# A decode-and-prompt attention layer on one core: unit outputs in four 32-column strips, decode transposes at the end of their step, five unread products taken out

## The reference

```python
o_a = gg[..., 0:1] * o_c + gg[..., 1:2] * o_s + gg[..., 2:3] * o_w     # compressed, selected, sliding window
s = (einsum('bqhc,bsc->bhqs', q_lat, c) + einsum('bqhr,bsr->bhqs', q_pe, kr)) * MLA_SCALE
o_lat = einsum('bhqs,bsc->bqhc', softmax(mask(s)), c)                   # latent attention
pa = (o_a * silu(ga)) @ w_proj_a;  pb = (o_b * silu(gb)) @ w_proj_b
h = sigmoid(ma) * pa + sigmoid(mb) * pb
y = x + rmsnorm(h @ w_out, norm_post)
```

## Time and profile before

| | |
|---|---|
| runs | 743.08, 744.10, 747.31 us, median 744.1 |
| span of the profiled execution | 739.6 us (its time outside the span is not recorded; the three runs are 3.5 to 7.7 us longer) |
| TensorE busy | 692.4 us of 739.6 |
| VectorE, ScalarE, GpSimd busy | 440.6, 211.5, 123.4 us |
| DMA | 170.27 MB, mean 230 GB/s |
| bound for "faster" or "slower" here | 0.5% of 744.1, 3.7 us |

### The profile page before, as it was taken

How to read it: one execution, slowest core, us unless ns; L and a number is a source line. 1 busy time by engine, 2 the same in 40 slices (tenths; PEclk the granted TensorE clock), 3 DMA queues, 4 the chain that set the end, 5 groups by cost and what they waited for, 6 DMA issues and landing times.

```text
span 739.6 us, 14391 instructions
## 1 busy us (share of the span) xinstructions
PE 692.4 (94%) x5305; PEld 443.7 (60%) x5305; DVE 440.6 (60%) x1233; ACT 211.5 (29%) x579; POOL 123.4 (17%) x130
## 2 busy tenths in 40 slices
PE   9997999999988979789999999899999999999996
PEld 4443444644555655467675676557778888885452
DVE  3297799478666756764654554542577565644244
ACT  0302215555334434433533442321110101110111
POOL 0343340113042230321412202320000000000000
PEclk9999999999999999999999999999999999999998
DMA  9999994951779999967755686996210303026011
GB/s 343 414 414 421 418 399 159 384 219 49 250 276 336 315 381 343 393 222 277 276 209 185 237 285 232 332 334 259 72 57 1 114 1 114 1 91 280 29 47 41
DMA packets 57367, 170.27 MB, mean 230 GB/s; under 512 B 7537, under 2 KB 7690, under 8 KB 50514
## 3 DMA queue, kind: packets, MB, share of 16 engines
q1 hardware_dynamic: 47352, 120.68, 45.1%
q0 software_dynamic: 9600, 48.38, 16.6%
q10 hardware_dynamic: 346, 0.29, 0.1%
HBM read 164.99 MB, written 8.52 MB: 235 GB/s over the span
## 4 chain that ended last, share of the span: by engine, by line
PE 75%; DMA 9%; DVE 5%; issue 5%; SPq 3%; ACT 2%; another core or an unknown queue 1%; DVEq 0%; ACTq 0%
PE bank L1423 18%; PE bank L855 7%; PE bank L1463 7%; PE bank L1266 7%; DMA W<-w_attn 4%; PE bank L1153 4%; PE bank L1132 3%; PE bank L1250 3%; PE bank L1235 3%; PE bank L1018 3%; PE bank L1140 3%; DMA projP<-x 2%; PE bank L1200 2%; PE bank L1455 2%; DMA ring<-latent 2%
## 5 line engine op out<-in xcount | busy, mean ns | idle before, releaser
L710 POOL DMA_INDIRECT KRR<-krT,idxi x64 | 61.2, 957 | 221.9 <-PE bank L1239 207.1
L855 PE MATMUL bank<-W,XG 128*128 128x494 f32 x192 | 85.2, 589 | 4.2 <-DMA W<-w_attn 3.7
L1484 ACT ACTIVATE projP<-bank 128x128 f32<-128x128 f32 (+5 forms) x87 | 33.9, 391 | 110.0 <-PE bank L1423 47.5
L2438 DVE TENSOR_TENSOR projP<-projP,bank 128x260 f32<-128x260 f32 x83 | 33.9, 422 | 45.1 <-PE bank L1423 44.4
L855 PEld LDWEIGHTS bank<-W,XG 128*128 128x128 f32 x192 | 35.8, 195 | 41.0 <-issue 39.8
L1266 PE MATMUL bank<-W 128*128 128x260 f32 x256 | 60.4, 389 | 0.0
L1484 ACT ACTIVATE W<-bank 128x512 f32<-128x512 f32 (+2 forms) x69 | 40.1, 582 | 69.8 <-PE bank L898 18.7
L1670 ACT ACTIVATE projP<-bank,projP 128x128 f32<-128x128 f32 (+3 forms) x96 | 49.7, 524 | 29.9 <-DVE projP L2140 29.5
L2140 DVE CUSTOM_DVE_ANT_0 bank<-bank,maskb 128x128 f32<-128x128 f32 (+3 forms) x96 | 45.8, 507 | 15.9 <-PE bank L1132 11.2
L1266 PEld LDWEIGHTS bank<-W 128*128 128x128 f32 x256 | 47.3, 190 | 10.4 <-issue 3.3
L1463 PE MATMUL bank<-ring,W 128*128 128x512 f32 x112 | 49.5, 594 | 1.3 <-issue 1.3
(11 more groups left out here) (439 smaller groups left out, 1145.7 us busy)
## 6 DMA issues: line engine op xcount, KB each, us to landing
ring<-latent SPq DMA_DIRECT2D x200, 256.0 KB
XG<-latent SPq DMA_DIRECT2D x56, 256.0 KB
W<-w_gate SPq DMA_DIRECT2D x12, 1024.0 KB, 4.7
W<-w_attn SPq DMA_DIRECT2D x16, 494.0 KB, 9.8
ring<-w_out SPq DMA_DIRECT2D x2, 2048.0 KB
o_win<-win SPq DMA_DIRECT2D x1, 4088.0 KB
W<-xT SPq DMA_DIRECT2D x1, 2080.0 KB, 11.2
projP<-x SPq DMA_DIRECT2D x1, 2048.0 KB
```

Of the source, the lines that this page charges most:

```text
L710: pool.indirect_dma_start(out=dst, out_offset=None, in_=src, in_offset=bass.IndirectOffsetOnAxis(ap=idxi[:, col:col + 1], axis=0)).then_in ...
L855: mm = pe.matmul(bank[2 * (u % 2) + n][:, 0:GW], XG[:, k * TOK + tl * P:k * TOK + (tl + 1) * P], w_part(half, k, n), start=(k == 0), stop= ...
L1484: return act.activation(dst, src, ACT.Copy, scale=scale)
```

## The change

Four edits:

1. `outputs`: each unit's output product is cut into two of 32 stationary columns, so that the pair has four strips of 32 partitions where it had two of 64. The moving operand (128 columns) and the sums are the same; 240 products become 480.
2. `dec_transposes(d)` stands at the end of step `d`, behind the transposes and the last keys, and no longer in step `d + 1` behind the scores; except in the steps of `TURN_LATE` (those before step 15 and those with a gate), where it stays. Twelve chunks move: those of steps 16, 17, 20, 22, 24, 28, 32, 36, 40, 42, 44 and 46. In 16, 24, 28, 32 and 36 it then stands right behind the last key block.
3. The five products of L1230 are gone.
4. On VectorE `read_out` stands ahead of `dec_fold` in a step.

```diff
+        TURN_LATE = {d for d in SOFT_at if d + 1 < 16 or d in G_at}
...
                 for kb in range(tl + 1):
-                    for e in range(2):
-                        mm = pe.matmul(bank[3][64 * e:64 * e + 64, 0:P], values(br, tl, kb, h + e), PTb[e][:, kb * P:(kb + 1) * P],
+                    for strip in range(4):
+                        e, lo = strip // 2, 32 * (strip % 2)
+                        mm = pe.matmul(bank[3][32 * strip:32 * strip + 32, 0:P], values(br, tl, kb, h + e)[:, lo:lo + 32], PTb[e][:, kb * P:(kb + 1) * P],
                                        start=(first and kb == 0), stop=(last and kb == tl))
...
-                if i2 == 0 and p2 in KEPT_BUSY:
-                    pe.matmul(bank[5][:, :], ident, qrT[:, 0:512], start=True, stop=True)
                 job_landed(pe, J_MLA + m)
...
-            KEPT_BUSY = (6, 12, 13, 14, 15)
...
                 if d < PAIRS:
                     scores(d)
-                if d - 1 in SOFT_at:
+                if d - 1 in TURN_LATE:
                     dec_transposes(d - 1)
...
                 if d in K_at:
                     dec_keys(d, 3)
+                if d in SOFT_at and d not in TURN_LATE:
+                    dec_transposes(d)
...
+                if 2 <= d < PAIRS + 2:
+                    read_out(d - 2)
                 if d in OUT_at:
                     dec_fold(OUT_at[d])
                 if d == 0:
                     new_tokens()
-                if 2 <= d < PAIRS + 2:
-                    read_out(d - 2)
```

## The result

The changed kernel took 762.66 us (median of four runs, 759.33 to 764.26), the kernel before beside it 744.68 (743.08 to 747.31): a ratio of 1.0227 with a 95% interval of 1.0188 to 1.0266. It is 18 us slower, where 2.9 us faster was forecast, and outside the range.

The account below looks back on a forecast made before the run. TensorE's time was taken to bound the kernel. The terms 6.4 - 1.2 - 3.7 + 1.4 gave 2.9 us faster, so a median of 744.1 - 2.9 = 741.2 us, with a range from 733 to 748.5.

Parts of the forecast that it names:

- the 1.36 us of the earlier trace: End of step 36: TensorE's idle time before the decode transpose, read as waiting for ScalarE's copy of the last key group.
- Edit 1, array time and tiling: Unit outputs: same array time, 0.11 us saved per tiling change at 58 of 66 handovers, 6.4 us faster; bounds 0 and 7.3.
- rival D: Unit outputs: four strips don't run side by side where key blocks accumulate into one bank; 13.4 us more, 754.6; chance 0.02.
- Edit 1, the number of instructions: Unit outputs: 480 more records, as many weight loads, cost 2.3 us or nothing; half taken, 1.2 us slower.
- Edit 2: Twelve moved decode transposes: scores queue behind them in steps with keys and step 22; net 3.7 us slower.
- the place in step 36: Transpose starts 2.8 us after the last key block as before; scores follow it, 1.7 to 2.5 us later than before.
- Rival A: Decode transposes: moving them costs nothing, so the waits' 4.0 us go; 737.2, down to 730.8; chance 0.30.
- B's 12 us: Rival B, decode transposes: all twelve moved groups delay the scores, 1.0 us each, 12 instead of 3.7; 749.5; chance 0.11.
- Edit 3: Five unread products, 4.8 us in all: removing them brings 1.4 us, as loads take the rest; bounds 0 and 4.8.
- Rival C: TensorE's clock falls more often without unread products and with unsplit idle time; three more falls cost 5.1 us, 746.3; chance 0.15.
- The sign that I had named: TensorE's clock: more than one new stretch at 1.2 GHz would show the prediction wrong.
- Theory S: From the experiments: the unit outputs' doubled instructions reach TensorE late, it stands still, and the clock falls behind it.

Follow-up runs that it names:

- filler: Kernel before with three waits on long-reached semaphores ahead of each unit output product, 271 more TensorE instructions: 753.2 us against 744.4, ratio 1.0103.
- group B: Runs timed together: edit 1 alone, and the changed kernel with one edit taken back in each of three; the kernel before took 723.0 us.
- group C: Runs timed together: changed kernel again, empty waits added, edits 2 and 4 alone, unread products out alone; the kernel before took 744.4 us.
- after_b: The changed kernel as it is, in a group where the kernel before took 720.9 us: 718.2 us, ratio 0.9965.
- turn_late: Changed kernel with all decode transposes one step later, as before the change: 716.2 us against 723.0 for the kernel before, ratio 0.9901.
- strips_only: Kernel before with edit 1 alone, four 32-column strips: 714.9 us against 723.0, ratio 0.9879.
- kept_out: Kernel before without the five unread products: 746.4 us against 744.4, ratio 1.0038.
- moved_only: Kernel before with edits 2 and 4, strips and unread products as before: 749.7 us against 744.4, ratio 1.0068.
- after_again: The changed kernel repeated word for word: 765.5 us against 744.4 for the kernel before, ratio 1.0268.

## Why the prediction was wrong, point by point

**What bounds the kernel** was read rightly: TensorE's time. But I read "issue" rows as a property of the code. The profile of before had 14.9 us of TensorE's idle time without a named releaser, in 20 pieces; the rows and the 1.36 us of the earlier trace rows are of this kind. All six profiles from the 744 us condition have 12 to 17 us of it, the fourteen from the 722 us condition 0 to 3.8. These rows, and the 18 us of "remote" on VectorE and ScalarE, were the sign that this execution ran in a condition in which TensorE's counts come late and part of them isn't recorded.

**Edit 1, array time and tiling: right in the 722 us condition.** 0.89 us from scores to outputs as forecast. Forecast -6.4 without the price for instructions, bounds 0 and -7.3; measured -5.4 to -8.1 in four groups of the 722 us condition. My rival D (strips not side by side) is out.

**Edit 1, the number of instructions: this is the step that failed.** I priced it at 1.2 us from 3.2 us of idle time in 666 records, with 2.3 as the upper bound. In the 722 us condition the price is near 0, within some 3 us. In the 744 us condition the filler's 271 empty instructions cost 8.8 us alone (by the interval of the ratio 3 to 12), more than the 2.3 that I had as the most for 960, and what the changed kernel loses beyond the other edits, with the strips' gain of 7.3 counted, is 18.0 to 21.1 - 5.3 - 2.0 + 7.3, again 18 to 21 us, for 960 instructions; a rest, not a measurement. The fault is in the way the bound was made: I took the mean idle time per record of one line as linear and complete, where the cost comes as late counts of TensorE's semaphores, up to 5.4 us each, for which ScalarE, VectorE and then TensorE itself wait, with falls of the clock behind them. The earlier trace rows alone held 6.3, 11.2 and 6.5 us in which TensorE wasn't busy. The quotient also mixed two stretches, 3.2 us from 440 to 510 and 666 records from 448 to 510; with the 821 records of the same stretch it is 1.9 us.

**Edit 2: right.** Forecast +3.7; measured, with edit 4 in it, +3.0 (group B) and +5.3 (group C), and the place in step 36 behaves as said. The 2.8 us from the last keys to the transpose there were themselves stretched by a late count: in after_b it is 1.48 us (405.92 to 407.40). Rival A, that it costs nothing, is out, and so is B's 12 us.

**Edit 3: wrong in sign, small in size.** Forecast -1.4; measured +1.3 in group B (with edit 4 in it, and not beyond its uncertainty) and +2.0 in group C (the products alone, 0.01% to 0.74%). The loads take part of the 4.8 us back as forecast: in the changed kernel the first latent scores of the last jobs wait for their load.

```profile
517.31 1.08 PE L1235 MATMUL bank<-ring,projP 128*32 128x128 f32 x32 [3.47 <-DMA ring<-latent]
...
523.32 0.92 PE L1235 MATMUL bank<-ring,projP 128*32 128x128 f32 x25 [1.53 <-DMA ring<-latent]
```

What I missed is that the clock takes more: turn_late, which differs from strips_only by the missing products and edit 4, has 13.7 us at 1.2 GHz where strips_only has 6.8, and kept_out has 23.9 where the profile of before has 10.2. At half speed 6.8 us more is a loss of 3.4. The profiled execution of turn_late is the slowest of its six, but the mean granted clock of all runs says the same: 0.985 against 0.989 for strips_only, and 0.977 (ten runs) for kept_out against 0.984 for the kernel before beside it. Over 740 us the latter is 5.0 us, and the rest of kept_out's time is 2.1 shorter.

**Rival C, the clock falls,** named the right mechanism with a chance of 0.15 and a wrong size. I allowed three more stretches and 5.1 us; there were six more with 30.8 us, 13.7 us of TensorE's work by the balance above. The sign that I had named, more than one new stretch, came true. The trigger that I gave (missing products, an idle piece no longer split by the scores) is a part of it. In group C the missing share of the clock times the span, a mean over all runs, is 12.3 us before, 14.4 in moved_only, 17.3 in kept_out, 19.2 in the filler and 30.3 in the changed kernel. So of its 21 us 18 go with the clock, and each of the three single changes moves it, though these parts needn't add up.

**The condition.** Nothing in the times of before (743.08 to 747.31) showed that the kernel also runs in 722 us; I had no run of the other level. In the 722 us condition the sum comes out (-2.9 forecast, -2.7 measured; its parts, -7.3 for the strips on the mean of four groups, +3.0 and +1.3, make -3.0), but that is luck in part: edit 3 came out 2.7 us worse than forecast, and what makes up for it is that the strips came out 0.9 better, edit 2 0.7 better, and that the 1.2 us for instructions weren't due there.

**What is shown and what is argued.** Shown: the level of 744 or 722 us changes the sign of the change; in the one, empty instructions cost 8.8 us, in the other nothing within some 3 us; the time is lost in stops of TensorE, VectorE and ScalarE that end with a late count of TensorE's, and in the clock behind them; the late counts grow with TensorE's added instructions and not with the other edits.

Argued: that the strips have the whole rest of the 18 to 21 us, since they never met this condition alone.

Theory S as it was put, that instructions reach TensorE late, is not borne out: at the three long stops the products whose counts are missing are on record as started before the stop. Nor do the instruction transfers bear it out. Of the stops of over 0.8 us, 7 of 10 begin between 0.5 us before and 2.5 us behind the start of one of the 16 KB transfers in the changed kernel (7 of 12 in after_again), where the 32 transfers of the stage cover under a third of its time in this way. But in the profile of before it is 2 of 8, in the filler 2 of 11, in moved_only 4 of 8 and in kept_out 4 of 9, and those transfers took about 1.1 us in either condition. The Trainium skill's page "Runtime: NRT & Kernel Launch", section "Instruction fetch mechanics", says that the engine fetches its instructions itself in blocks of 16 KB and that crossing a block is mostly hidden. The 722 us condition agrees (0 to 3.8 us of unnamed idle time); for the 744 us condition no run here shows what holds the counts back.

What makes the condition stays open as well. One rival stands untested: the recording itself. Each time here is of an execution whose clock was recorded, and in the 744 us condition the record has lost about a fifth of the semaphore counts. No run shows whether the counts come late in an execution that isn't recorded.

## What to carry to other kernels

Look at TensorE's idle time with no named releaser, and at "remote" on the engines that read its banks, before pricing anything: where they are more than a few us, the profile may be from a condition in which an added instruction costs far more than its array time, and the kernel should be timed in other groups before a change is judged. Price extra instructions by an empty filler of the same number, not by a mean over records. And when an idle time is named after VectorE or ScalarE, see whether that engine had itself been standing still: then look for what it waited for, here a count of TensorE's own.

The version to keep is the kernel before with the strips alone: 714 to 716 us against 721 to 724, 1.0% faster over four groups (ratios 0.9879, 0.9930, 0.9880, 0.9903), and faster than the changed kernel in the group that ran both (715.5 against 718.2). It has not been timed in the 744 us condition, where its 960 instructions may cost more than the strips bring.

## What the runs showed of the hardware that was not expected

- The same kernel has two levels, 744 and 722 us (3%), each within 0.8% in a group of 4 to 19 runs; the first 200 us of the changed kernel are alike in both, the attention stage is not.
- At the higher level 42 to 74 of TensorE's some 340 recorded semaphore counts in the attention stage come over 1 us after the latest start of a product that makes them, up to 5.4 us, and often several within 0.2 us; at the lower level two of some 5500 do, at most 1.10 us. The record has 7627 to 7785 counts of all engines at the one, 9457 to 9613 at the other.
- 271 instructions that wait for long-reached semaphores in TensorE's stream cost 8.8 us at the higher level (32 ns each on average, in a few stops) and, together with the strips, nothing measurable at the lower.
- A change of the array's tiling from 32 to 64 columns and back costs about 0.11 us each; taking out the 66 of them brought 5.4 to 8.1 us.
- Taking out five products that nobody reads, 0.96 us each, made the kernel 1.3 to 2.0 us slower in the medians (both near their uncertainty), and its mean granted clock lower (0.977 against 0.984 in the ten and nineteen runs of group C).
